# A differential attention whose values are computed with the queries on the partitions, and whose norm becomes a factor per partition

## The chip, the cores and the metric

The kernel runs on one core of one Trainium2 chip. The metric is the device time of one execution in microseconds; three runs of the kernel before gave 1177.27, 1177.3 and 1177.53, with a median of 1177.3 us. The engines named below are TensorE (PE, with its weight loads as PEld), VectorE (DVE), ScalarE (ACT), GpSimd (POOL) and SyncE (SP), which issues most of the DMAs.

## The reference, cut to what matters

The program is two transformer blocks over 512 tokens with a model width of 1024. The second block has a sparse attention of 8 heads and a differential attention of 4 heads. The change is in the differential attention, between the product with the values and the output projection:

```python
def rmsnorm(x, g):
    xf = x.astype(f32)
    y = xf * lax.rsqrt(jnp.mean(xf * xf, axis=-1, keepdims=True) + EPS)
    return (y * g.astype(f32)).astype(x.dtype)

# diff_attention, for a block of 128 queries; 4 heads, values of width 128
p = probs(q1, k1f) - lam * probs(q2, k2f)
o = jnp.einsum('bhqs,bshe->bqhe', p, vf)
...
o_d = rmsnorm(o_d, g_diff_sub[layer]) * (1.0 - lam_init)
mix = jnp.concatenate([o_a, o_d], axis=-1)
y = jnp.einsum('bsc,cd->bsd', mix, w_out[layer])
```

The norm is taken for each query and each head over the 128 columns of that head.

## The kernel before, in words

Every engine has a program written out by hand; the order of the work on an engine is the order of its code, and the engines meet at semaphores. Nothing is scheduled by a planner.

The attention stage (about 642 to 787 us of the span) is a loop over 32 tiles, `step(n)` for n from -2 to 32, which each engine has in its own version. Tiles 0 to 15 are the differential ones: head h = n // 4 and query block tb = n % 4, with (tb + 1) * 128 keys. Tiles 16 to 31 are pairs of sparse heads. In step n, TensorE computes the scores of tile n + 2 (L925), a part of a projection for the sparse attention (`project_part`, up to n = 16) or pieces of the output projection (`out2_piece`, from n = 20), transposes the probabilities of tile n (`turn`, L939) and multiplies those of tile n - 1 with the values (`values`, L963 for differential tiles, L967 for sparse ones). VectorE normalises tile n (`normalise`), and scales and masks the scores of tile n + 2 (`shift`, L1979); top-k work and rotary embeddings for later tiles lie between its steps. ScalarE copies the transposed probabilities out of PSUM (`keep_turned`, L1371) and takes the exponentials of tile n + 2 (`exp`, L1356). GpSimd splits each weight chunk of 128x1024 into a high and a low part (L411, L414) when TensorE has freed its slot, and computes the low part of heads 0 and 1 (`head_low2`, L462).

The outputs of one differential head are gathered in one PSUM bank, transposed: the 128 columns of the head on the partitions, the 512 queries along the free dimension. Since the norm is a mean over the partitions, it goes through TensorE. For head h:

- after its last tile, `keep_output` on ScalarE copies the bank to SBUF (`kept[h]`, L1381) and squares it (`sq`, L1383);
- `head_sums` on TensorE (L654, L656, at the end of steps 5, 9, 16 and 17) sums the squares of each query over the partitions with four matmuls of one column each, onto an eps that is scaled by the softmax totals; this gives four columns of the bank NB;
- `head_roots` on ScalarE (steps 9 and 17, two heads at a time) takes the roots from NB, and VectorE takes the reciprocals into `rn` (L2027, steps 12 and 18);
- `norm_spread` on TensorE (L677, at the steps of `SPREAD_AT`: 14, 15, 19, 20) turns each column of reciprocals into a row over all partitions of NB;
- VectorE multiplies `kept[h]` with the gain and with NB (L2032, same steps), into `kept[h]` for heads 0 and 1 and into NB for heads 2 and 3;
- ScalarE rounds the result to the high part `xh` (L1400, steps 16, 17, 19 and 20), and the low part `xl` is computed on GpSimd (heads 0 and 1) or on VectorE (L2017, steps 20 and 21).

NB is one bank: each user waits until the one before it has let go (semaphores `bc_used`, `xl_ready`).

## Time and profile before

| | |
|---|---|
| median of three runs | 1177.3 us |
| the profiled execution | 1177.28 us, of which the span of the trace is 1175.6 us |
| PE busy, of the span | 1156.2 us (98%) |
| DVE / ACT / POOL busy | 611.4 / 292.3 / 719.4 us |
| TensorE clock granted, mean | 0.996 of full |
| chain that ended last | PE 93%, DVE 5%, ACT 1%, issue 1% |

The profile gives one execution with the start and duration of every instruction. A step of the attention stage is found in it by its width: the scores and exponentials of block tb are (tb + 1) * 128 columns wide, so four widths come round for each head. Times below are from the start of the span; "idle before" is how long an engine had done nothing, followed by the instruction whose end let it go on.

### The profile page before, as it was taken

How to read it: one execution, taken by the hardware profiler on the slowest of the kernel's cores; microseconds unless marked ns; L12 is line 12 of the kernel's file. 1: busy time of each engine (PE TensorE's matmuls, PEld its weight loads, DVE VectorE, ACT ScalarE, POOL GpSimd, SP SyncE). 2: the span in 40 equal slices, each digit the busy share in tenths (PEclk: the TensorE clock that was granted, in tenths of full speed). 3: DMA queues.
4: the chain of work that ended last, by engine and by line, in shares of the span. 5: the costliest groups of instructions: out<-in, count | busy, mean ns of one | idle time of the engine just before them, and what ended most of it. 6: DMA issues, size and time to landing. Idle time of an engine off the chain costs nothing.

```text
span 1175.6 us, 15616 instructions
## 1 busy us (share of the span) xinstructions
PE 1156.2 (98%) x5400; PEld 931.0 (79%) x5400; DVE 611.4 (52%) x1001; ACT 292.3 (25%) x576; POOL 719.4 (61%) x440
## 2 busy tenths in 40 slices
PE   7999999999999999999999999999999999999997
PEld 5887788888888888888777776777888888888886
DVE  4989874540015444448689778847554001454114
ACT  5144162210002121120202346546421000221111
POOL 7879958656666566656556333225876666665660
PEclk9999999999999999999999999999999999999998
DMA  7321223323232232324342221112232232322312
GB/s 269 114 90 36 90 72 131 102 95 102 89 107 89 94 104 90 107 90 134 108 126 90 88 78 57 30 55 73 76 120 90 95 103 89 107 89 94 104 36 72
DMA packets 35761, 111.25 MB, mean 95 GB/s; under 512 B 4993, under 2 KB 7169, under 8 KB 35713
## 3 DMA queue, kind: packets, MB, share of 16 engines
q1 hardware_dynamic: 32352, 105.40, 27.2%
q10 hardware_dynamic: 3360, 5.21, 1.6%
q8 instruction: 30, 0.49, 0.2%
q14 instruction: 19, 0.15, 0.0%
HBM read 102.99 MB, written 2.10 MB: 89 GB/s over the span
## 4 chain that ended last, share of the span: by engine, by line
PE 93%; DVE 5%; ACT 1%; issue 1%; DMA 0%; DVEq 0%; SPq 0%; ACTq 0%
PE bank L560 26%; PE bank L562 25%; PE bank L561 25%; PE bank L925 2%; PE bank L591 2%; PE bank L593 2%; PE bank L592 2%; DVE bank L1596 2%; PE bank L625 1%; PE bank L617 1%; PE bank L939 1%; PE bank L618 1%; PE bank L967 1%; PE bank L883 1%; PE bank L963 1%
## 5 line engine op out<-in xcount | busy, mean ns | idle before, releaser
L414 POOL TENSOR_TENSOR wl<-raw,wh 128x1024 fp32r<-128x1024 f32 x188 | 455.1, 2421 | 15.7
L411 POOL TENSOR_SCALAR wh<-raw 128x1024 fp32r<-128x1024 f32 x188 | 203.1, 1080 | 391.9 <-PE bank L562 273.3
L560 PE MATMUL bank<-xh,wh 128*128 128x512 f32 x776 | 307.9, 397 | 0.4 <-ACT va L1332 0.4
L562 PE MATMUL bank<-xh,wl 128*128 128x512 f32 x776 | 302.4, 390 | 0.0
L561 PE MATMUL bank<-xl,wh 128*128 128x512 f32 x776 | 302.3, 390 | 0.0
L560 PE MATMUL bank<-uh,wh 128*128 128x512 f32 (+1 forms) x560 | 215.4, 385 | 0.0
L562 PE MATMUL bank<-uh,wl 128*128 128x512 f32 (+1 forms) x560 | 214.5, 383 | 0.0
L561 PE MATMUL bank<-ul,wh 128*128 128x512 f32 (+1 forms) x560 | 214.5, 383 | 0.0
L560 PEld LDWEIGHTS bank<-xh,wh 128*128 128x128 f32 x776 | 145.6, 188 | 45.6 <-issue 16.2
L1795 DVE TENSOR_TENSOR ul<-tmb,uh 128x512 f32 x64 | 124.6, 1947 | 90.2 <-ACT uh L1277 90.2
L562 PEld LDWEIGHTS bank<-xh,wl 128*128 128x128 f32 x776 | 145.6, 188 | 31.1
L561 PEld LDWEIGHTS bank<-xl,wh 128*128 128x128 f32 x776 | 145.8, 188 | 29.0 <-issue 0.2
L1276 ACT ACTIVATE tmb<-tmp 128x512 f32<-128x512 f32 x64 | 40.5, 633 | 413.1 <-DVE tmp L1792 413.1
L561 PEld LDWEIGHTS bank<-ul,wh 128*128 128x128 f32 x560 | 105.2, 188 | 20.9 <-issue 0.2
L560 PEld LDWEIGHTS bank<-uh,wh 128*128 128x128 f32 x560 | 105.2, 188 | 20.6 <-issue 0.2
L562 PEld LDWEIGHTS bank<-uh,wl 128*128 128x128 f32 x560 | 105.2, 188 | 20.6
L1792 DVE SCALAR_TENSOR_TENSOR tmp<-bank,rb 128x512 f32<-128x512 f32 x64 | 44.0, 688 | 70.7 <-PE bank L562 66.0
L1596 DVE SCALAR_TENSOR_TENSOR bank<-gpad,cols,bank 128x512 f32<-128x512 f32 x98 | 66.6, 744 | 0.0
L1806 DVE TENSOR_TENSOR x<-bank,x 128x512 f32 x8 | 5.5, 692 | 78.1 <-PE bank L562 78.1
L1808 DVE COPY y<-bank 128x512 f32 x8 | 5.5, 692 | 78.1 <-PE bank L562 78.1
L1277 ACT ACTIVATE uh<-tmp 128x512 f32 x64 | 39.6, 618 | 0.0
L591 PE MATMUL bank<-wh,xh 128*128 128x512 f32 x96 | 38.0, 395 | 0.0
(278 smaller groups left out, 1234.8 us busy)
## 6 DMA issues: line engine op xcount, KB each, us to landing
raw<-wstream SPq DMA_DIRECT2D x188, 512.0 KB, 3.3
x<-xT SPq DMA_DIRECT2D x8, 256.0 KB, 4.8
out<-x SPq DMA_DIRECT2D x16, 128.0 KB, 1.7
qi<-ropey ACTq DMA_DIRECT2D x16, 64.0 KB, 2.1
qd<-ropey ACTq DMA_DIRECT2D x16, 64.0 KB, 2.3
kd<-ropey ACTq DMA_DIRECT2D x16, 64.0 KB, 2.1
qa<-ropey SPq DMA_DIRECT2D x16, 64.0 KB, 2.0
ka<-ropey SPq DMA_DIRECT2D x16, 64.0 KB, 2.0
```

What stands on the lines that cost most here:

```text
L411: nc.gpsimd.tensor_scalar(wh[c][:], raw[c][:], 1.0, 1.0, ALU.mult, ALU.mult).then_inc(high_ready, 1)
L414: nc.gpsimd.tensor_tensor(wl[c][:], raw[c][:], wh[c][:].bitcast(F32), ALU.subtract).then_inc(split_ready, 1)
L560: mm(out, wh_, mh, start=start, stop=False)
L561: mm(out, wh_, ml, start=False, stop=False)
L562: return mm(out, wl_, mh, start=False, stop=stop)
L591: mm(out, xh[:, k, ts], wh[s][:, ws], start=k == 0, stop=False)
L592: mm(out, xh[:, k, ts], wl[s][:, ws], start=False, stop=False)
L1276: A(tmb[c][:], tmp[c][:], ACT.Square).then_inc(square_ready, 1)
L1277: A(uh[:, bass.ds(r * 4 + c, 1), :].rearrange("p a n -> p (a n)"), tmp[c][:], ACT.Square).then_inc(uh_ready, 1)
L1596: ins = V.scalar_tensor_tensor(out=out, in0=src, scalar=w, in1=acc, op0=ALU.mult, op1=ALU.add)
L1792: V.scalar_tensor_tensor(out=tmp[c][:], in0=bank[c][:], scalar=0.0, in1=rb[:], op0=ALU.max, op1=ALU.mult).then_inc(evacuated, 1)
L1795: V.tensor_tensor(ul[:, bass.ds(r * 4 + c, 1), :].rearrange("p a n -> p (a n)"), tmb[c][:], uh[:, bass.ds(r * 4 + c, 1), :].rearrange("p a ...
```

## The change

The product with the values is turned round: the transposed probabilities are now the stationary operand and the values the moving one, so that a bank holds the 128 queries of each block on the partitions and the columns of the head along the free dimension, once for each of the four query blocks. The mean over a head's columns is then a sum along the free dimension. ScalarE takes it with an accumulator output, in four squares of 128 columns for each head in place of one of 512. One small instruction on VectorE (`head_mean`, steps 9 and 17) adds the scaled eps for two heads; the root and the reciprocal follow, and VectorE multiplies each head with its reciprocals as a factor per partition (`natural_o`, steps 12, 13, 18 and 19). TensorE then transposes the head into NB (`head_turn`, at the steps where the spreads stood), and the gain, which is now again a factor per partition, is applied where NB is read: by ScalarE in a copy back to `kept[h]` for heads 0 and 1 (steps 14 and 15), and by the readers of NB for heads 2 and 3.

```diff
-            def head_sums(h):
-                at = 4 * (h % 2)
-                ...
-                mm(NB[:, at:at + TB], ident[:], scaled_eps[:, TB * h:TB * h + TB], start=True, stop=False)
-                for t in range(TB):
-                    last = mm(NB[:, at + t:at + t + 1], sq[h % 2][:, t * P:t * P + P], inv[:, 1:2],
-                              start=False, stop=t == TB - 1)
+            def head_turn(h):
+                pe.wait_ge(head_scaled, h + 1)
+                if h == 0:
+                    pe.wait_ge(bc_used, 8)
+                elif h < 3:
+                    pe.wait_ge(head_used, h)
+                else:
+                    pe.wait_ge(xl_ready, 3 * KT + 3)
+                for t in range(TB):
+                    last = nc.tensor.transpose(NB[:, t * P:t * P + P], kept[h][:, t * P:t * P + P], ident[:])
+                last.then_inc(head_turned, 1)
...
-                        last = mm(out, vd[:, j, h * P:h * P + P], pT[n % 2][0][:, b], start=j == 0, stop=j == tb)
+                        last = mm(out, pT[n % 2][0][:, b], vd[:, j, h * P:h * P + P], start=j == 0, stop=j == tb)
... TensorE, step(n)
-                if n in SPREAD_AT and SPREAD_AT[n] < 3:
-                    h = SPREAD_AT[n]
-                    pe.wait_ge(bc_used, 8 + h)
-                    norm_spread(8 + h)
+                if n in TURN_AT and TURN_AT[n] < 3:
+                    head_turn(TURN_AT[n])
...
-                if n in (5, 9):
-                    head_sums(n // 4 - 1)
-                if n in (16, 17):
-                    head_sums(n - 14)
... ScalarE, keep_output(h)
-                if h >= 2:
-                    act.wait_ge(sums_done, 6 + h)
                 A(kept[h][:], bank[1 if h == 3 else 6][:], ACT.Copy).then_inc(o_kept, 1)
                 act.wait_ge(o_kept, h + 1)
-                A(sq[h % 2][:], kept[h][:], ACT.Square).then_inc(head_sq, 1)
+                for t in range(TB):
+                    A(sq[h % 2][:, t * P:t * P + P], kept[h][:, t * P:t * P + P], ACT.Square,
+                      accum_out=head_sum[:, TB * h + t:TB * h + t + 1]).then_inc(head_sq, 1)
... ScalarE, step(n)
+                    if h < 2:
+                        act.wait_ge(head_used, h + 1)
+                        A(xh[:, 4 + h], kept[h][:], ACT.Copy).then_inc(xh_ready, 1)
+                    else:
+                        act.wait_ge(head_turned, h + 1)
+                        A(xh[:, 4 + h], NB[:], ACT.Copy, scale=diff_gain[:]).then_inc(xh_ready, 1)
                 if n + 2 < TILES:
                     exp(n + 2)
+                if n in TURN_AT and TURN_AT[n] < 2:
+                    h = TURN_AT[n]
+                    act.wait_ge(head_turned, h + 1)
+                    A(kept[h][:], NB[:], ACT.Copy, scale=diff_gain[:]).then_inc(head_used, 1)
... VectorE, step(n)
                 if 0 <= n < TILES:
                     normalise(n)
+                if n in (9, 17):
+                    b = n // 17 * 8
+                    dve.wait_ge(head_sq, 4 + b + 8)
+                    dve.wait_ge(eps_scaled, b // 4 + 2)
+                    V.scalar_tensor_tensor(out=sd[:, 0:8], in0=head_sum[:, b:b + 8], scalar=1.0 / P,
+                                           in1=scaled_eps[:, b:b + 8], op0=ALU.mult, op1=ALU.add).then_inc(head_mean, 1)
                 if n + 2 < TILES:
                     shift(n + 2)
                 if n in (12, 18):
...
-                    V.reciprocal(rn[:, 0:8], sd[:, 0:8]).then_inc(rn_ready, 2)
-                if n in SPREAD_AT:
-                    h = SPREAD_AT[n]
-                    dve.wait_ge(bc_done, 9 + h)
-                    V.scalar_tensor_tensor(out=kept[h][:] if h < 2 else NB[:], in0=kept[h][:], scalar=diff_gain[:],
-                                           in1=NB[:], op0=ALU.mult, op1=ALU.mult).then_inc(bc_used, 1)
+                    link(V.reciprocal(rn[:, 0:8], sd[:, 0:8]))
+                if n in (12, 13, 18, 19):
+                    h = n - 12 if n < 14 else n - 16
+                    natural_o = kept[h][:].rearrange("p (a b) -> p a b", a=TB)
+                    V.tensor_tensor(natural_o, natural_o, rn[:, h % 2 * TB:h % 2 * TB + TB].unsqueeze(2)
+                                    .to_broadcast([P, TB, P]), ALU.mult).then_inc(head_scaled, 1)
```

The low part of heads 2 and 3 is now computed from NB times the gain. Semaphore counts elsewhere fall by four, since four spreads are gone; no other order changes.

The order of the instructions moves at three places that matter. On ScalarE, steps 14 and 15 before, from the copy of tile 14's transposed probabilities (L1371) to the copy of tile 16's:

```order
L1371 ACTIVATE tmp_84<-bank 128x384 [waits turned,pv_done]
L1356 ACTIVATE probs_115,soft<-probs_115,soft 128x128 [waits shifted] x2
L1371 ACTIVATE tmb_87<-bank 128x512 [waits turned,pv_done]
L1356 ACTIVATE probs_122,soft<-probs_122,soft 128x256 [waits shifted]
L1356 ACTIVATE probs_123,soft<-probs_123,soft 128x256 [waits shifted]
L1371 ACTIVATE tmp_84<-bank 128x128 [waits turned,pv_done]
```

and now, where L1365 is that copy, L1350 the exponential and L1404 the new copy from NB:

```order
L1365 ACTIVATE tmp_84<-bank 128x384 [waits turned,pv_done]
L1350 ACTIVATE probs_116,soft<-probs_116,soft 128x128 [waits shifted] x2
L1404 ACTIVATE tmb_85<-bank,diff_gain 128x512 [waits head_turned]
L1365 ACTIVATE tmb_87<-bank 128x512 [waits turned,pv_done]
L1350 ACTIVATE probs_123,soft<-probs_123,soft 128x256 [waits shifted]
L1350 ACTIVATE probs_124,soft<-probs_124,soft 128x256 [waits shifted]
L1404 ACTIVATE tmb_86<-bank,diff_gain 128x512 [waits head_turned]
L1365 ACTIVATE tmp_84<-bank 128x128 [waits turned,pv_done]
```

Each of the two steps now ends with a read of NB, and TensorE's second turn waits for the first.

On VectorE, step 17 before, from the second half of the normalisation of tile 17 (L2007, L2008) over the shift of tile 19 (L1979) to the rotary products (L1502):

```order
L2007 RECIPROCAL soft<-soft 128x1 [waits exp_done]
L2008 TENSOR_SCALAR probs_123<-probs_123,soft 128x256 [waits dve_chain]
L1979 ISA probs_115,soft<-bank,work 128x512 [waits scores_done,turned]
L1979 ISA soft 128x1
L1979 ISA probs_115,soft<-bank,work 128x512 [waits scores_done]
L1979 ISA soft 128x1
L1502 TENSOR_TENSOR tmp_82<-bank,sinr 128x512 [waits chunk_done]
L1502 TENSOR_TENSOR tmp_83<-bank,cosr 128x512
```

and now, with the mean (L2023) in it:

```order
L2007 RECIPROCAL soft<-soft 128x1 [waits exp_done]
L2008 TENSOR_SCALAR probs_124<-probs_124,soft 128x256 [waits dve_chain]
L2023 SCALAR_TENSOR_TENSOR sd<-head_sum,scaled_eps 128x8 [waits eps_scaled,head_sq]
L1979 ISA probs_116,soft<-bank,work 128x512 [waits scores_done,turned]
L1979 ISA soft 128x1
L1979 ISA probs_116,soft<-bank,work 128x512 [waits scores_done]
L1979 ISA soft 128x1
L1502 TENSOR_TENSOR tmp_82<-bank,sinr 128x512 [waits chunk_done]
L1502 TENSOR_TENSOR tmp_83<-bank,cosr 128x512
```

The mean moved in ahead of the shift of tile 19, and it waits for `head_sq`, the squares of head 3.

On TensorE, from the values of tile 15 (L963) in step 16 to the sums at the end of step 17, before:

```order
L963 MATMUL bank<-tmb_87,vd 128x128 x3
L654 MATMUL bank<-scaled_eps,ident 128x4 [waits eps_scaled,head_sq,bc_used]
L656 MATMUL bank<-inv,sq_75 128x1 x4
L925 MATMUL bank<-ka,qa 128x512 [waits shifted] x2
L939 MATMUL bank<-ident,probs_122 128x128 [waits pT_ready,probs_ready]
L939 MATMUL bank<-ident,probs_122 128x128
L939 MATMUL bank<-ident,probs_123 128x128 [waits pT_ready,probs_ready]
L939 MATMUL bank<-ident,probs_123 128x128
L967 MATMUL bank<-tmp_84,va 64x128 [waits pT_ready,o_kept]
L967 MATMUL bank<-vd,va 64x128
L654 MATMUL bank<-scaled_eps,ident 128x4 [waits eps_scaled,head_sq]
L656 MATMUL bank<-inv,sq_76 128x1 x4
```

and now, where L964 and L968 are the values, L926 the scores and L940 the transposes:

```order
L964 MATMUL bank<-vd,tmb_87 128x128 x3
L926 MATMUL bank<-ka,qa 128x512 [waits shifted] x2
L940 MATMUL bank<-ident,probs_123 128x128 [waits pT_ready,probs_ready]
L940 MATMUL bank<-ident,probs_123 128x128
L940 MATMUL bank<-ident,probs_124 128x128 [waits pT_ready,probs_ready]
L940 MATMUL bank<-ident,probs_124 128x128
L968 MATMUL bank<-tmp_84,va 64x128 [waits pT_ready,o_kept]
L968 MATMUL bank<-vd,va 64x128
```

The two sums, L654 with the four one-column matmuls of L656, are gone, and nothing has taken their place.

## Rows read from the trace of the kernel before

**Rows 1.** PE by stretch: start:end, length, busy (instructions), granted clock, DMA share, GB/s.

```profile
645.00:700.00 55.00, 55.00 (x289) 1.00 0.26 77
...
710.00:715.00 5.00, 3.80 (x20) 1.00 0.34 110
```

**Rows 2.** Timeline of DVE, steps 11-14: start, us, engine, instruction, [idle before, releaser].

```profile
701.50 0.69 DVE L1883 TENSOR_TENSOR ropey<-tmp,tmp 128x512 f32<-128x512 f32 x1
...
705.06 0.56 DVE L1979 CUSTOM_DVE_ANT_0 probs<-bank,mask 128x384 f32<-128x384 f32 x1 [1.30 <-PE bank L925]
...
706.02 0.20 DVE L2027 RECIPROCAL rn<-sd 128x8 f32<-128x8 f32 x1
...
708.17 2.31 DVE L1997 SCALAR_TENSOR_TENSOR probs<-probs,soft 128x256 f32<-128x256 f32 x1
...
714.25 0.62 DVE L1997 SCALAR_TENSOR_TENSOR probs<-probs,soft,probs 128x384 f32<-128x384 f32 x1
```

**Rows 3.** Timeline of PE, steps 14 and 15.

```profile
714.92 0.55 PE L939 MATMUL bank<-ident,probs 128*128 128x128 f32 x3 [0.71 <-DVE probs L1997]
...
716.48 0.65 PE L677 MATMUL bank<-ident,rn 128*128 128x128 f32 x4
```

**Rows 4.** Timeline of DVE, steps 17 to 19.

```profile
725.37 0.69 DVE L1979 CUSTOM_DVE_ANT_0 probs<-bank,work 128x512 f32<-128x512 f32 x1 [1.95 <-PE bank L925]
...
727.99 0.42 DVE L2008 TENSOR_SCALAR probs<-probs,soft 128x384 f32<-128x384 f32 x1
...
729.38 1.71 DVE L1883 TENSOR_TENSOR ropey<-tmp,tmp 128x512 f32<-128x512 f32 x1
...
731.80 0.16 DVE L2007 RECIPROCAL soft<-soft 128x1 f32<-128x1 f32 x1
```

**Rows 5.** Timeline of PE, steps 18 and 19.

```profile
728.48 1.18 PE L939 MATMUL bank<-ident,probs 128*128 128x128 f32 x6 [0.18 <-DVE probs L2008]
...
732.70 1.08 PE L939 MATMUL bank<-ident,probs 128*128 128x128 f32 x8
```

**Rows 6.** PE by stretches of 1 us, steps 18 and 19.

```profile
730.00:731.00 1.00, 1.00 (x10) 0.50 0.00 0
...
732.00:733.00 1.00, 1.00 (x7) 0.66 0.00 0
```

**Rows 7.** Timeline of PE, step 5.

```profile
676.25 0.28 PE L654 MATMUL bank<-scaled_eps,ident 128*128 128x4 f32 x2
676.39 1.03 PE L656 MATMUL bank<-inv,sq 128*128 128x1 f32 x8
677.36 0.49 PE L925 MATMUL bank<-kd,qd 64*128 64x128 f32 x4
```

**Rows 8.** Timeline of ACT, steps 14 and 15, from the exponentials.

```profile
715.96 0.39 ACT L1356 ACTIVATE probs<-probs,soft 128x128 f32<-128x128 f32 x1
...
716.34 0.39 ACT L1356 ACTIVATE probs<-probs,soft 128x128 f32<-128x128 f32 x1
...
719.05 0.60 ACT L1371 ACTIVATE tmb<-bank 128x512 f32<-128x512 f32 x1 [2.23 <-PE bank L939]
```

**Rows 9.** Timeline of POOL, steps 12 and 18.

```profile
707.82 2.39 POOL L414 TENSOR_TENSOR wl<-raw,wh 128x1024 fp32r<-128x1024 f32 x1
...
729.27 1.27 POOL L462 TENSOR_TENSOR xl<-tmb,xh 128x512 fp32r<-128x512 f32 x1 [2.33 <-ACT xh L1400]
```

**Rows 10.** Source view of ACT's L1218, a copy with a scale: ns min/median/max.

```profile
L1218 ACT ACTIVATE vg<-bank,rn x4: 681/690/692, 77.6 to 79.5; 128x512 f32<-128x512 f32 x4
```

**Rows 11.** Timeline of ACT, steps 16 and 17, from the squares.

```profile
725.91 0.63 ACT L1383 ACTIVATE sq<-vd 128x512 f32<-128x512 f32 x1
...
730.51 0.72 ACT L1356 ACTIVATE probs<-probs,soft 128x512 f32<-128x512 f32 x1
```

**Rows 12.** Source view of ACT's L1159, squares without and with a scale.

```profile
L1159 ACT ACTIVATE sq<-x x24: 614/632/635, 161.9 to 829.4; 128x512 f32<-128x512 f32 x24
L1159 ACT ACTIVATE sq<-x,cols x8: 707/708/709, 440.5 to 516.5; 128x512 f32<-128x512 f32 x8
```

More of the change, by code:

```diff
@@ L1019, in step @@
                     turn(n)
-                if n in SPREAD_AT and SPREAD_AT[n] == 3:
-                    pe.wait_ge(xl_ready, 3 * KT + 3)
-                    norm_spread(11)
+                if n in TURN_AT and TURN_AT[n] == 3:
+                    head_turn(3)
                 if n >= 1:
                     values(n - 1)
-                if n in (5, 9):
-                    head_sums(n // 4 - 1)
-                if n in (16, 17):
-                    head_sums(n - 14)
             for n in range(-2, TILES + 1):
@@ L1531, in norm_factor @@
             def norm_factor(i, keep=None):
[L1533 removed]
+                dve.wait_ge(sd_ready, i + 1 if i < 8 else i + 3)
                 if i:
```

66 lines of the change are left out of this document (29 added, 37 removed).

## The prediction

> **What bounds the kernel now.** I read the busy time and the granted clock by stretch first, then the waits and the timeline of each engine for the attention stage, step by step. TensorE sets the end nearly everywhere. From 645 to 700 us it is busy for all of the 55.00 us at the full clock, and only in steps 12 to 14 does it show a hole, 3.80 us busy in 5 [rows 1]. So a microsecond taken from TensorE before 700 us is a microsecond off the end, and what the other engines do there is hidden unless it makes TensorE late. There are two places in this stage where TensorE follows somebody else, and both are in the way of the change.
>
> The first is steps 12 to 14. VectorE was idle for 1.30 us until TensorE's scores of tile 14 let it go at 705.06, and from there it runs without a pause to the probabilities of tile 14, which end at 714.87 [rows 2]. TensorE waits for them, 0.71 us, and starts its transposes at 714.92 [rows 3]. The second is steps 17 to 19. VectorE's shift of tile 19 starts at 725.37 as soon as TensorE's scores are there, its instructions then follow each other to 731.80, where the normalisation of tile 19 starts [rows 4], and TensorE's transposes start at 728.48, on a release by VectorE, and at 732.70 [rows 5]. TensorE's clock is down to half there: 0.50 from 730 to 731, 0.66 from 732 to 733 [rows 6]. After 733 us TensorE is the bound again. What the change costs or brings is therefore its effect on the start of the transposes of tile 19.
>
> **The change part by part: TensorE's sums of heads 0 and 1.** In step 5 the sums start at 676.25 and the next scores at 677.36 [rows 7], so one `head_sums` holds TensorE for 1.11 us. Those of heads 0 and 1 (steps 5 and 9) lie where TensorE never waits [rows 1]. Both go: -2.22 us. The values with swapped operands are the same number of matmuls of 128x128 on the same fp32 data, and the transposes of `head_turn` are four of the same 128x128 as those of `norm_spread`; both are taken at no change.
>
> **ScalarE's squares of heads 0 to 2** become four of 128 columns with an accumulator. I price them below; they cost well under 1 us more for a head, and at steps 4, 8 and 12 ScalarE next waits for TensorE's transposes, as it does for 2.23 us before 719.05 [rows 8]. Nothing. If that cover were gone they would cost 0.6 to 0.9 us for each head.
>
> **VectorE's factors of heads 0 and 1.** The mean in step 9 is one instruction of 8 columns, 0.2 us by the reciprocal of 8 columns [rows 2], and lies before a shift that waits for TensorE: nothing. In step 12 the reciprocal is now waited for (0.1 us) and a product of 128x512 follows. Its operands are all in SBUF; such a product took 0.69 us when alone [rows 2], and I charge 0.65, since the next instruction overlaps its end. That is 0.75 us on the chain to tile 13. But there the chain runs into GpSimd: the 256 columns of tile 13 took 2.31 us from 708.17, ending at 710.48, while 384 columns take 0.62 at 714.25 [rows 2], and GpSimd's split of a chunk ran until 710.21 [rows 9]. An SBUF-only instruction of VectorE stood until GpSimd was done. GpSimd is released by the same TensorE that releases VectorE, so both come 2.22 us earlier, and 0.75 us of arriving later at the same hold cost nothing. If the hold were not there, they would cost up to 0.75. The product of step 13 comes behind it and has no cover: +0.65 us on the start of the transposes of tile 14. The two products of VectorE that go, in steps 14 and 15, lie where TensorE does not wait for it: nothing back.
>
> **ScalarE's copies of heads 0 and 1.** TensorE turns head 1 in step 15, where its spread started at 716.48 [rows 3]. It now needs NB read, and the reader is ScalarE, behind the exponentials of tile 16. These start at 715.96 and 716.34, 0.38 apart [rows 8], so the copy starts at 716.72. A copy of 512 columns from PSUM with a scale per partition took 0.69 us [rows 10]. It ends at 717.41, and TensorE stands for 717.41 - 716.48 = 0.93 us with a projection, the transposes of tile 15 and all later work queued behind. All these times hang on the transposes of tile 14, so they shift together. From below, 0.8 (a copy as short as the 0.60 of the transposed tile [rows 8]); from above 1.0. I take +0.93. The copy of head 1 has 2 us of idle time around it and costs nothing.
>
> At the start of step 16 this makes -2.22 + 0.65 + 0.93 = **-0.64 us**.
>
> **Steps 16 to 19.** The sums of heads 2 and 3 go too, 2.22 us of TensorE's time. But the mean of heads 2 and 3 stands on VectorE ahead of the shift of tile 19, and it waits for the last square of head 3. ScalarE starts these squares at 725.91 [rows 11], since head 3's output comes late, after the exponentials of tile 18. One square of 512 columns without a scale takes 0.63 us, with one 0.71 [rows 12]; exponentials of 128 columns, with a pointer and an accumulator, follow each other every 0.38 us [rows 8]. Without the pointer (0.08 less) four squares take 4 x 0.30 = 1.2 us, with it 1.5. I take 1.25. VectorE gets on at 725.91 + 1.25 + 0.2 for the mean = 727.4, where the shift stood at 725.37: **2.0 us later** (1.8 to 2.4). Behind the mean are queued the shift of tile 19, for which TensorE's scores of tile 20 wait, then the rotary products and the normalisation of tile 18, for which its transposes wait. What TensorE saved in steps 16 and 17 it spends standing there: the saving is worth nothing.
>
> In step 18 the awaited reciprocal and the product of head 2 add 0.1 + 0.65 = 0.75 us ahead of the rotary sum and the normalisation of tile 19. GpSimd's hold, 1.27 us from 729.27 [rows 9], made the rotary sum at 729.38 last 1.71 us [rows 4]; it follows ScalarE's rounding of head 1, which comes 0.6 us later, and meets the normalisation of tile 18 instead, due at 727.99 + 2.0 = 730.0 [rows 4]. It is paid once either way. So the normalisation of tile 19 starts at 731.80 + 2.0 + 0.75 = 734.55, and its first half is ready about 0.65 us on (reciprocal, and a factor over 512 columns), at 735.2, where the transposes of tile 19 began at 732.70 [rows 5]: **+2.5 us**. ScalarE is no rival to that: its exponentials of tile 19 move from 730.51 [rows 11] by only 0.6. From there TensorE has no wait that the new order adds: the gain on NB makes the low part an instruction of the same length, and for heads 2 and 3 VectorE's product between spread and rounding is gone, which gives slack but no time.
>
> **The clock.** TensorE now stands for some 3 us between the values of tile 16 and the scores of tile 20, and again before tiles 18 and 19. In before, where it stood for far less between small matmuls, the clock was at half rate for some 3 us, about 729.5 to 732.7 [rows 6], and a half-rate stretch costs half its length where TensorE is the bound. If one ends before 735.2 it is hidden; if it begins there it costs 1.6. I take +0.7.
>
> The Trainium skill (TensorE: Matmul & The Clock Gate, section HAM oscillation — how this bites in real kernels) has the rule that standing sends the array to half rate and that the work after the gap then starts cold. That rule speaks against this change, and by it the full 1.6 us would fall due, for a time of 1180.7 us; the trace of before shows such a dip, but not where it falls when the gap is longer.
>
> **The sum.** -0.64 + 2.5 + 0.7 = +2.56 us. The profiled execution took 1177.28 us, 1.7 more than its span of 1175.6; the median of the runs is 1177.3. So 1177.28 + 2.56 = **1179.8 us**.
>
> **Rivals.**
>
> *The wait in step 17 is covered, not slower.* If head 3's squares were done before VectorE comes to the mean, the sums of all four heads count: -4 x 1.11 + 0.65 + 0.93 = -2.9 us, 1174.4 us. This decides if the squares end by 725.4. For it speaks that ScalarE was idle before step 16 and that TensorE gets to head 3's values earlier in its own order; against it, that the squares stood at 725.91 with nothing between them and their input but the exponentials of tile 18 [rows 11], so they would have to come 1.8 us earlier.
>
> *The cost of the wait is smaller.* Squares as quick as 0.25 us, no dip of the clock behind step 19 and TensorE's transposes of tile 18 and scores of tile 21 catching up: 1.2 less for the clock and squares, and with the copies at their lower bound about +0.6, 1177.9 us. What speaks for it is that the half-rate time of before also cost something in these steps and may be spared now.
>
> *The clock stays down and the squares are long.* Four squares at 0.38 (+0.3), step 12's product not covered (+0.6) and 1.6 in place of 0.7 for the clock: +4.4, 1181.7 us. The dip of before [rows 6] speaks for it; GpSimd's hold speaks against the second part.
>
> **Chances.** Forecast 0.57, its own range 1178.8 to 1181.0; covered wait 0.08; smaller cost 0.18; clock and long squares 0.17. The range to hold the time 8 times in 10 is 1175.8 to 1182.6. A difference of 0.2% (2.35 us) is about what a measurement tells from no change: the bounds are 1174.95 and 1179.65. The forecast lies just above the upper one, so about 0.33 of its 0.57 counts as slower, with all of the last case: slower 0.50, within 0.42, faster 0.08.
>
> **What would show it.** Right: in the trace of after, VectorE's mean of step 17 has some 2 to 4 us of idle time before it, released by ScalarE's squares; TensorE waits about 0.9 us in step 15 on ScalarE's copy, and a few microseconds in step 18 on VectorE; everything to step 11 stands 2.2 us earlier; the transposes of tile 19 start near 732.70 - 0.64 + 2.5 = 734.6, and from there to the end the shift is constant up to the clock. Wrong: no wait at the mean (then faster), a shift at step 11 that is not 2.2 us, values with swapped operands that take another time, or a half-rate stretch in steps 20 and 21 or none at all.

## The result: 1181.6 us, slower by 0.37%

| | before | after |
|---|---|---|
| median (runs) | 1177.3 us (7) | 1181.62 us (7), 1181.2 to 1182.71 |
| profiled execution | 1177.28 us, span 1175.6 | 1182.71 us, span 1181.0 |
| ratio of the times | | 1.0037, 95% interval 1.0028 to 1.0046 |

The prediction was 1179.8 us with a range of 1175.8 to 1182.6. The direction and the range held; the forecast's own range (1178.8 to 1181.0) did not. By the medians the difference is 4.3 us and in the profiled executions 5.4 us, where the sum said 2.56. The profiled execution of after is the slowest of its seven, 1.1 us above the median and just outside the range. What follows explains that execution. Four of the seven lie at 1181.2 to 1181.62 with a mean granted clock of 0.994 to 0.996, three at 1182.17 to 1182.71 with 0.993 to 0.994. That agrees with a part of the half-rate time below being there in some executions and not in others.

The page of after, its first lines: span, and busy time of each engine. TensorE has 40 instructions less and is busy 1.4 us less, in a span that is 5.4 us longer: it stands idle 6.8 us more. The four sums that are gone were 4.4 us of its work, so some 3 us of the 1154.8 are the same work at a lower clock (an estimate from these two numbers).

```profile
span 1181.0 us, 15563 instructions
...
PE 1154.8 (98%) x5360; PEld 929.6 (79%) x5360; DVE 611.9 (52%) x1003; ACT 296.2 (25%) x606; POOL 718.6 (61%) x440
```

TensorE in after by stretch (length, busy, granted clock, DMA), for [rows 1] and [rows 6]. The stretch to 700 us now has a hole of 1.05 us, and there are two stretches at half rate (a granted clock of 0.50 is 1.2 GHz, 1.00 is 2.4 GHz) where before had one: 3.4 us from 717 to 721 and 6.8 us from 731 to 738, against 3.4 in before (the length is the clock that is missing in each microsecond, divided by a half and added up).

```profile
645.00:700.00 55.00, 53.95 (x273) 1.00 0.27 82
...
717.00:718.00 1.00, 0.53 (x3) 0.68 0.00 0
718.00:719.00 1.00, 1.00 (x5) 0.50 0.06 16
...
731.00:732.00 1.00, 0.87 (x3) 0.51 0.01 4
736.00:737.00 1.00, 1.00 (x8) 0.50 0.00 0
737.00:738.00 1.00, 1.00 (x7) 0.58 0.00 0
```

The timeline of TensorE in after, its waits in steps 10 to 19 (start, duration, instruction, idle time before it and who ended it), for [rows 3] and [rows 5]. L940 are the transposes of a tile's probabilities (tiles 10, 13, 14, 15, 18 and 19 here), L658 those of `head_turn`, L926 the scores.

```profile
698.27 0.55 PE L940 MATMUL bank<-ident,probs 128*128 128x128 f32 x3 [1.05 <-DVE probs L1997]
...
709.86 0.44 PE L940 MATMUL bank<-ident,probs 128*128 128x128 f32 x2 [0.49 <-DVE probs L1997]
...
714.85 0.55 PE L940 MATMUL bank<-ident,probs 128*128 128x128 f32 x3 [1.30 <-DVE probs L1997]
...
717.47 1.09 PE L658 MATMUL bank<-ident,tmb 128*128 128x128 f32 x4 [0.99 <-ACT tmb L1404]
...
720.86 0.60 PE L940 MATMUL bank<-ident,probs 128*128 128x128 f32 x4
...
730.61 1.40 PE L926 MATMUL bank<-ka,qa 64*128 64x128 f32 x4 [2.92 <-DVE soft L1979]
733.98 1.54 PE L940 MATMUL bank<-ident,probs 128*128 128x128 f32 x6 [1.97 <-DVE probs L2008]
...
738.22 1.04 PE L940 MATMUL bank<-ident,probs 128*128 128x128 f32 x8
```

VectorE in after, for [rows 2] and [rows 4]. L2023 is the new mean: VectorE stands 3.17 us ahead of it in step 9 and 3.82 us in step 17, until ScalarE's squares are there. The two long L1997 and the long L2008 ran beside an instruction of GpSimd: those of 695.83 and 732.47 beside the two shown below, that of 708.15 beside L417 from 707.14 to 709.53.

```profile
692.60 0.17 DVE L2023 SCALAR_TENSOR_TENSOR sd<-head_sum,scaled_eps 128x8 f32<-128x8 f32 x1 [3.17 <-ACT sq L1376]
...
695.83 2.38 DVE L1997 SCALAR_TENSOR_TENSOR probs<-probs,soft 128x384 f32<-128x384 f32 x1
...
708.15 1.66 DVE L1997 SCALAR_TENSOR_TENSOR probs<-probs,soft 128x256 f32<-128x256 f32 x1
...
729.73 0.17 DVE L2023 SCALAR_TENSOR_TENSOR sd<-head_sum,scaled_eps 128x8 f32<-128x8 f32 x1 [3.82 <-ACT sq L1376]
...
732.47 1.46 DVE L2008 TENSOR_SCALAR probs<-probs,soft 128x384 f32<-128x384 f32 x1
```

GpSimd in after, for [rows 9].

```profile
695.41 2.38 POOL L417 TENSOR_TENSOR wl<-raw,wh 128x1024 fp32r<-128x1024 f32 x1
...
732.45 1.26 POOL L465 TENSOR_TENSOR xl<-tmb,xh 128x512 fp32r<-128x512 f32 x1 [3.02 <-ACT xh L1395]
```

ScalarE in after: the first and the last of head 3's four squares, and the table load behind them, for [rows 11]. They follow each other every 0.30 us, 728.42 to 729.70.

```profile
728.42 0.31 ACT L1376 ACTIVATE sq<-vd 128x128 f32<-128x128 f32 x1
...
729.31 0.29 ACT L1376 ACTIVATE sq<-vd 128x128 f32<-128x128 f32 x1
...
729.72 1.28 ACT L1416 ACT_TABLE_LOAD   x1
```

The best single ruler is ScalarE's copy of each tile's transposed probabilities, which follows TensorE closely. Its start, minus that of the same tile in the kernel before (us; the kernels of the other columns come in the next section, "repairs" is the kernel with three repairs):

| tile | after | mean moved | copies on VectorE | no sums | repairs | repairs, filled |
|---|---|---|---|---|---|---|
| 5 | +0.04 | -0.08 | +0.22 | +0.03 | +0.46 | +0.24 |
| 6 | -0.99 | -1.11 | -0.80 | -0.87 | -0.57 | -0.79 |
| 10 | -0.77 | -2.15 | -0.58 | -1.77 | -1.62 | -1.84 |
| 14 | -0.07 | -1.45 | +0.10 | -1.80 | -1.52 | -1.74 |
| 15 | +2.50 | -0.40 | +0.12 | -1.80 | -1.37 | -1.59 |
| 17 | +3.15 | +0.25 | +0.77 | -1.80 | -0.72 | -0.94 |
| 19 | +5.46 | +0.99 | +3.89 | -1.06 | -0.06 | -0.84 |
| 22 to 28 | +5.4 | +1.4 | +3.9 | -1.0 | -0.1 | -0.7 |

The row of tile 5 is a start-up difference of the execution; a column is read down from it. Each column is one execution of its kernel.

### The profile page after: what moved, and what is told of

It reads as the page before. It is cut to its first block, busy times and chain, and to the rows that moved or that the text cites. A ratio compares the mean times of both kernels' runs of the same rounds, so it can differ in the third digit from the quotient of the medians.

```text
span 1181.0 us, 15563 instructions
## 1 busy us (share of the span) xinstructions
PE 1154.8 (98%) x5360; PEld 929.6 (79%) x5360; DVE 611.9 (52%) x1003; ACT 296.2 (25%) x606; POOL 718.6 (61%) x440
## 4 chain that ended last, share of the span: by engine, by line
PE 92%; DVE 5%; ACT 1%; issue 1%; DMA 0%; DVEq 0%; SPq 0%; ACTq 0%
PE bank L563 25%; PE bank L565 25%; PE bank L564 25%; PE bank L594 2%; PE bank L596 2%; PE bank L595 2%; DVE bank L1596 2%; PE bank L926 2%; PE bank L628 1%; PE bank L940 1%; PE bank L620 1%; PE bank L621 1%; PE bank L968 1%; PE bank L884 1%; PE bank L964 1%
## 5 line engine op out<-in xcount | busy, mean ns | idle before, releaser
L417 POOL TENSOR_TENSOR wl<-raw,wh 128x1024 fp32r<-128x1024 f32 x188 | 454.5, 2417 | 15.7
L414 POOL TENSOR_SCALAR wh<-raw 128x1024 fp32r<-128x1024 f32 x188 | 203.0, 1080 | 397.4 <-PE bank L565 278.2
```

The source lines that it names most:

```text
L414: nc.gpsimd.tensor_scalar(wh[c][:], raw[c][:], 1.0, 1.0, ALU.mult, ALU.mult).then_inc(high_ready, 1)
L417: nc.gpsimd.tensor_tensor(wl[c][:], raw[c][:], wh[c][:].bitcast(F32), ALU.subtract).then_inc(split_ready, 1)
```

## The experiments

Theory 1, formed from the trace of after: VectorE's in-order wait for ScalarE's squares at the mean loses the saving of step 9 and costs 2 us in step 17. Rival A: the squares on ScalarE themselves are the cost, wherever the mean stands. Rival B: TensorE's clock in step 15 falls whatever waits there. Rival C: VectorE is the engine that is late in steps 14 and 15. The kernel before ran beside each kernel; its median was 1177.3 to 1177.5 us each time.

**mean_late.** The mean of both steps goes behind the shift:

```diff
@@ VectorE, step(n)
-                if n in (9, 17):
-                    ... the mean into sd, two waits ahead of it
                 if n + 2 < TILES:
                     shift(n + 2)
@@ VectorE, the loop over n, behind qk_second
+                if n in (9, 17):
+                    ... the same lines
```

> The changed kernel with VectorE's mean of steps 9 and 17 behind the shift (and behind the second rotary part or the score's maxima) of the same step. Theory 1 (VectorE's in-order wait for ScalarE's squares, ahead of a shift that TensorE and ScalarE wait for, lost the saving of step 9, about 1.0 us, and cost 2.0 us in step 17, and pushed step 18's instructions under GpSimd's hold and into the half-rate stretch, up to 2.3 us more): the median falls from 1181.6 to between 1176.5 and 1178.7 us; tile 10 to 13 stand 1.8 us ahead of the kernel before instead of 0.8. Rival A (the squares themselves on ScalarE, four of 0.3 us in place of one of 0.7, are the cost, wherever the mean stands): 1181 to 1182. Rival B (TensorE's clock stays low after the wait of head_turn(1) in step 15 and that alone makes the loss): at most 0.5 us less, 1181.1 or more.

Measured: 1179.19 us (1178.31 to 1180.77, 11 runs), ratio to before 1.0017 (1.0008 to 1.0026): 2.4 us back. Tiles 10 to 13 stand 2.1 us ahead of before (expected 1.8). Rivals A and B, each as the whole cause, fall; but the time is above the range of theory 1. What is left shows in TensorE's timeline: step 14 waits 1.32 us for VectorE, step 15 0.99 us for ScalarE's copy, and in step 18 the wait did not go. It changed its owner, from VectorE to ScalarE. The clock, 1.00 at 717, does not fall behind the wait of step 15 in this execution, which is one of the quicker ones (1178.64 us, mean clock 0.995); four of the eleven took 1180.03 to 1180.77 us at 0.993 to 0.994, as they would with one such stretch more.

```profile
713.48 0.55 PE L940 MATMUL bank<-ident,probs 128*128 128x128 f32 x3 [1.32 <-DVE probs L1997]
...
716.09 0.63 PE L658 MATMUL bank<-ident,tmb 128*128 128x128 f32 x4 [0.99 <-ACT tmb L1404]
...
728.73 1.51 PE L940 MATMUL bank<-ident,probs 128*128 128x128 f32 x6 [2.91 <-ACT tmb L1365]
```

**mean17_late.** The mean of step 17 alone is moved.

> The changed kernel with the mean of step 17 alone behind that step's shift; step 9 as in the changed kernel. Theory 1: the 2.0 us of step 17 come back, and of step 18's 2.3 us what hangs on it; 1177.5 to 1179.7 us, and about 1 us more than with both moved. Rival A (squares) and B (clock after step 15): within 0.5 us of 1181.6.

Measured: 1180.03 us (1179.37 to 1181.57, 11 runs), ratio 1.0022 (1.0013 to 1.0031). So step 17 gives 1.6 us back and step 9 another 0.8, the order that theory 1 has, but 0.3 us above its range. TensorE's wait of 1.06 us before the transposes of tile 10 is still there, as it was in after.

**copies_dve.** ScalarE's copies of heads 0 and 1 go to VectorE, everything else as in after:

```diff
@@ ScalarE, step(n)
-                if n in TURN_AT and TURN_AT[n] < 2:
-                    ...
-                    A(kept[h][:], NB[:], ACT.Copy, scale=diff_gain[:]).then_inc(head_used, 1)
@@ VectorE, step(n), behind shift and the reciprocals
+                if n in TURN_AT and TURN_AT[n] < 2:
+                    h = TURN_AT[n]
+                    dve.wait_ge(head_turned, h + 1)
+                    V.tensor_scalar(kept[h][:], NB[:], diff_gain[:], None, ALU.mult).then_inc(head_used, 1)
```

> The changed kernel with the copies of heads 0 and 1 out of NB (times the gain) on VectorE in steps 14 and 15, ahead of nothing that TensorE waits for, in place of ScalarE. Theory 1 with the forecast's step (TensorE's head_turn(1) waits 0.99 us for ScalarE's copy, which stands behind an exponential): the copy comes earlier by 0.5 to 1 us, TensorE's wait of step 15 goes below 0.5 us, and if the half-rate stretch at 717 to 721 us hangs on that wait it goes too; median 1178.5 to 1181.0. Rival B (the clock falls there whatever waits): the wait goes, the clock stays at half rate, 1180.7 to 1181.7. Rival C (VectorE is the engine that is late there, so 0.4 us more on it in steps 14 and 15 costs as much as ScalarE gives): 1181.5 to 1183.

Measured: 1180.81 us (1180.54 to 1181.52, 7 runs), ratio 1.0028 (1.0017 to 1.004): 0.8 us less than after, and rival C falls. The time alone would also fit rival B; the trace decides against it. In it far more happened: TensorE's wait of step 15 is gone, its clock is 1.00 from 717 to 721, and tile 15 stands 2.4 us earlier than in after. Both the 0.99 us and, in the traced executions, the 1.6 us at half rate hung on ScalarE's copy. But a part, 0.8 us, is given back between tiles 17 and 19, where the mean and GpSimd's hold are still in the way: behind a wait for the mean, L2004 of tile 18 is held again.

```profile
727.35 0.17 DVE L2019 SCALAR_TENSOR_TENSOR sd<-head_sum,scaled_eps 128x8 f32<-128x8 f32 x1 [3.82 <-ACT sq L1376]
...
730.09 1.46 DVE L2004 TENSOR_SCALAR probs<-probs,soft 128x384 f32<-128x384 f32 x1
```

**no_sums.** The kernel before without the matmuls that sum the squares:

```diff
@@ TensorE, head_sums(h)
-                mm(NB[:, at:at + TB], ident[:], scaled_eps[...], start=True, stop=False)
-                for t in range(TB):
-                    last = mm(NB[:, at + t:at + t + 1], sq[h % 2][...], inv[:, 1:2], ...)
+                last = mm(NB[:, at:at + TB], ident[:], scaled_eps[...], start=True, stop=True)
```

> The kernel before with the sixteen one-column matmuls that sum the squares of the four heads left out (the norm's factor is then computed from epsilon alone). It prices what the change removes from TensorE with nothing put in its place. Theory (in-order TensorE waits for its own work in steps 5 and 9, each 1.0 to 1.1 us, in steps 16 and 17 as well if nothing else is late there): 2.0 us less at step 10, and 2 to 4 us less at the end: 1173.3 to 1175.3. Rival (waits for VectorE and ScalarE behind those steps take the saving back): 1176 to 1177.3.

Measured: 1176.3 us (1175.25 to 1177.18, 11 runs), ratio 0.9987 (0.9978 to 0.9996). The saving is 1.0 us of the 4 us of work removed (1.03 for each head by [rows 7]). In the trace it is 1.8 us up to step 10, near the 2.0 foreseen; in steps 16 and 17 it is nothing, and between tiles 18 and 19 0.8 us go back. Its timeline of TensorE says why: where the sums were, it waits for ScalarE.

```profile
724.80 0.39 PE L654 MATMUL bank<-scaled_eps,ident 128*128 128x4 f32 x2 [1.30 <-ACT sq L1380]
...
726.68 1.51 PE L936 MATMUL bank<-ident,probs 128*128 128x128 f32 x6 [1.07 <-ACT tmb L1368]
```

And its clock falls around the second of these waits and stays down for 6.8 us instead of 3.4 (TensorE by stretches of 1 us, first, second and last of the half rate):

```profile
725.00:726.00 1.00, 0.60 (x6) 0.77 0.76 266
...
726.00:727.00 1.00, 0.32 (x2) 0.50 0.56 225
...
732.00:733.00 1.00, 1.00 (x10) 0.82 0.44 107
```

The 0.8 us do not go back in every execution: five of the eleven took 1175.25 to 1175.57 us at a mean clock of 0.996 to 0.998, 1.8 to 2.1 us less than before, and six took 1176.3 to 1177.18 at 0.995 to 0.996, the traced one among them.

This gave **theory 2**: from step 16 to step 18 ScalarE is the bound, already in the kernel before. From 723.25 to 735 us of the trace of before it has no idle time; two exponentials of 384 columns, head 3's copy and squares, a table load, the copies of tile 17 and a second table load follow each other. The sums lay in TensorE's wait for it and, by this theory, kept the clock up. Then, in after, the four squares, 1.28 us where one took 0.63 [rows 11], are paid in full, and an idle TensorE pays again in clock. (The copy of tile 17 is that of its transposed probabilities.)

**fixed** has three repairs: mean_late, copies_dve, and the product of head 1 in step 14 instead of 13 (`if n in (12, 14, 18, 19)`).

> The changed kernel with all three repairs on VectorE's side: the mean of steps 9 and 17 behind the shift, the copies of heads 0 and 1 on VectorE, and the product of head 1 in step 14 instead of 13. Theory 2 (in steps 16 to 18 ScalarE, busy without a gap from 723 to 736 us, is what TensorE waits for, and the four squares of head 3 make its chain 0.65 us longer than before): up to tile 16 the whole saving stands, 2.0 us, at tile 18 1.3 to 1.4 us are left, and TensorE's half-rate stretch, 6.5 us long in the kernel with the mean moved and 3.3 us before, takes another 1.0 to 1.4 us: median 1176.8 to 1178.0. Rival (theory 1 alone: the waits that were repaired were the whole loss, nothing of the kind is left behind them): 1175.0 to 1175.7.

Measured: 1177.16 us (1176.86 to 1178.01, 11 runs), ratio 0.9997 (0.9988 to 1.0006): no difference to before, and 4.5 us less than after. Theory 2's number and its course fit, the rival's 1175.7 does not (the lowest run is 1176.86): read from tile 5 on, it is 2.1 us ahead at tile 10, 1.8 at tile 15, 1.2 at tile 17 and 0.5 at tile 19. The wait in step 18 is 2.92 us for ScalarE's copy of tile 17:

```profile
727.76 1.51 PE L940 MATMUL bank<-ident,probs 128*128 128x128 f32 x6 [2.92 <-ACT tmb L1365]
```

and the half rate runs from 726 to 733:

```profile
726.00:727.00 1.00, 0.00 (x0) 0.62 0.94 373
...
732.00:733.00 1.00, 1.00 (x7) 0.50 0.27 66
```

**fixed_fill** adds five matmuls of 512 columns, whose result nobody reads, in that wait:

```diff
@@ TensorE, step(n), behind scores(n + 2)
+                if n == 18:
+                    pe.wait_ge(head_used, 2)
+                    for _ in range(5):
+                        mm(NB[:], ones[:], mask[:], start=True, stop=True)
```

> The kernel with the three repairs, and five matmuls of 512 columns by constants into the free bank NB, computed for nothing, on TensorE in step 18 behind scores(20), in the wait for ScalarE. Theory 2 (an idle TensorE in that wait brings the half-rate stretch forward and makes it longer; the one-column sums that the change removed had kept it busy there): the stretch starts later or is shorter by 2 us or more, and the median is 0.6 to 1.2 us below that of the three repairs alone. Rival (the stretch comes whatever TensorE does there): no gain, 0 to 0.3 us more.

Measured: 1176.6 us (1176.29 to 1176.72, 11 runs), ratio 0.9991 (0.9982 to 1.0): 0.56 us less than without them, and no run of one kernel reaches into those of the other. The gain is just below the 0.6 to 1.2 expected, since the five (4.56 us) overrun the wait: turn(18) starts at 728.95 where ScalarE had released it at 727.4. No stretch of the trace is below full clock, which is more than was expected; the mean clock is 0.997 to 0.999 in all eleven runs and 0.995 in all eleven of fixed, and the runs lie within 0.43 us instead of 1.15.

```profile
724.55 4.56 PE L1014 MATMUL bank<-mask,ones 128*128 128x512 f32 x10
728.95 0.82 PE L940 MATMUL bank<-ident,probs 128*128 128x128 f32 x6
...
731.86 1.25 PE L940 MATMUL bank<-ident,probs 128*128 128x128 f32 x8 [0.28 <-DVE probs L2008]
```

**sums_head3** is the kernel before with the sums of head 3 alone kept.

> The kernel before with the one-column matmuls of heads 0, 1 and 2 left out and those of head 3 kept (the norm's factor of the three is then computed from epsilon alone). Theory 2 (in step 17 these sums lie in a wait for ScalarE and only keep TensorE's clock up): 0.6 to 0.9 us faster than with all four left out, that is 1175.3 to 1175.7, with a half-rate stretch of 3 to 5 us instead of 6.4. Rival (they cost their 1.0 us in step 17 too): 1 us slower than with all left out, 1177.3.

Measured: 1175.42 us (1175.24 to 1177.15, 11 runs), ratio 0.9986 (0.9977 to 0.9995). With 1.0 us more of work for TensorE than no_sums it is not slower: the lowest runs are 1175.24 and 1175.25, and the traced executions 1175.32 and 1176.3. So the sums of head 3 cost nothing, and the rival (1177.3) falls. In these two traces the same transposes start at the same time but here at full clock (0.85 us in place of 1.51), and the half rate is 727 to 731:

```profile
726.68 0.85 PE L939 MATMUL bank<-ident,probs 128*128 128x128 f32 x6 [0.18 <-ACT tmb L1371]
```

The medians differ by 0.9 us, but that is which of two groups the middle run fell in. Here eight runs took 1175.24 to 1175.87 us (mean clock 0.996 to 0.998) and three 1176.59 to 1177.15 (0.995); in no_sums five and six. The means are 1175.8 and 1176.1 and the intervals overlap, so that the small sums make the long stretch rarer is not shown.

**fixed_one** puts one square for each head back on ScalarE, with two reductions on VectorE ahead of each mean (`reduce_sum` of `sq[h]` as 128x4x128 into four columns of `head_sum`). ScalarE also waits for the first mean ahead of the squares of heads 2 and 3.

> The kernel with the three repairs, and ScalarE's four squares of 128 columns with sums per head put back to one square of 512 columns; VectorE sums them (two reductions of 128x4x128) just ahead of the mean. Theory 2: ScalarE's chain in step 16 gets 0.65 us shorter, so turn(18) starts 0.6 us earlier and the median falls by 0.5 to 0.8 us against the three repairs alone, unless the two reductions (0.6 us each) on VectorE, behind the second rotary part in step 17, delay turn(18) by as much: turn(18) would then wait for VectorE. Rival (ScalarE's squares are not on the path): no change or 0.3 us more.

Measured: 1178.12 us (1177.38 to 1178.52, 11 runs), ratio 1.0005 (0.9996 to 1.0014): 1.0 us slower than fixed. The exception in the expectation came true, so this says nothing against theory 2. Two reductions take 1.40 us in line, and turn(18) now waits for VectorE; in step 9 the other two push the normalisation of tile 10 (L1993 here) under GpSimd's hold again (2.29 us, and TensorE waits 1.06).

```profile
726.29 1.40 DVE L2060 TENSOR_REDUCE head_sum<-sq 128x4 f32<-128x512 f32 x2
...
728.47 1.54 PE L940 MATMUL bank<-ident,probs 128*128 128x128 f32 x6 [2.76 <-DVE probs L2004]
```

**one3_fill** keeps that for head 3 alone (one square, one reduction in step 17), on the kernel with three repairs and four filling matmuls.

> The kernel with the three repairs and the matmuls of constants in step 18 (four instead of five), and for head 3 alone one square of 512 columns on ScalarE with one reduction of 0.7 us on VectorE behind the second rotary part, in place of four squares with sums. The reduction for head 3 lies where VectorE waited for ScalarE (0.36 us), so little is late behind it. Theory 2 (ScalarE's chain from step 16 on sets turn(18) and turn(19)): 0.3 to 0.7 us below the 1176.6 us of the kernel with four squares and matmuls of constants. Rival (VectorE is the bound there as well, by its products and GpSimd's hold): within 0.2 us of 1176.6.

Measured: 1176.3 us (1176.06 to 1177.24, 11 runs), ratio 0.9990 (0.9981 to 0.9999); 0.3 us below fixed_fill, which was measured beside other runs of before (medians 1177.37 and 1177.45); the ratios to before, 0.9990 and 0.9991, hardly differ. At tile 17 it is 0.6 us better than fixed_fill, both read from tile 5, as theory 2 has it, but at turn(19) 0.3 is left: the rival is right there. (Turn(18) itself is no test, since in both kernels it follows the filling matmuls, five of them in one and four in the other.) VectorE's rotary sum is held by GpSimd and turn(19) waits for VectorE:

```profile
728.24 1.76 DVE L1885 TENSOR_TENSOR ropey<-tmp,tmp 128x512 f32<-128x512 f32 x1
...
731.46 1.25 PE L940 MATMUL bank<-ident,probs 128*128 128x128 f32 x8 [0.81 <-DVE probs L2010]
```

**piece_fill** fills the wait with needed work, the first piece of the output product out of step 20, between one and two filling matmuls (`PIECES = {18: 1, 19: 0, 20: 1, 21: 2, ...}`).

> The kernel with the three repairs, where TensorE's wait of step 18 (2.9 us) is filled with work that is needed: the first piece of the output product (three matmuls of 512 columns, 0.7 to 0.8 us) is moved from step 20 to step 18, with one matmul of constants ahead of it and two behind. Theory 2 (the wait is for ScalarE, and TensorE is the bound again from step 20 on, so work moved into the wait is saved): 0.5 to 0.8 us below the 1176.6 us of the kernel filled with constants alone. Rival (step 20 has a wait of its own that takes it back): 1176.4 to 1176.8.

Measured: 1176.35 us (1176.09 to 1176.5, 11 runs), ratio 0.9989 (0.9980 to 0.9998), 0.25 us below fixed_fill (with the same reservation as above), half of the least that was expected and just below the rival's 1176.4. turn(19) cannot start before ScalarE has copied tile 18 and VectorE has normalised tile 19, so a part of the piece's time came back as a wait:

```profile
731.90 1.25 PE L940 MATMUL bank<-ident,probs 128*128 128x128 f32 x8 [1.23 <-ACT vd L1371]
```

**best** joins the two, with one filling matmul on each side of the piece.

> Both of these together (one square for head 3, the first piece of the output product in step 18, one matmul of constants ahead of it and one behind). Theory 2: the two add up, 1175.2 to 1175.8. Rival: 1176.2 or more, the bound of the steps 18 and 19 being VectorE and GpSimd's hold.

Measured: 1177.0 us (1175.84 to 1177.16, 11 runs), ratio 0.9990 (0.9981 to 1.0). The two do not add up, as the rival had it. Turn(19) starts at 731.38, as early as in no other kernel with the change, but TensorE has then stood 1.75 us for VectorE, and the clock is at half rate from 733 us on:

```profile
731.38 1.25 PE L940 MATMUL bank<-ident,probs 128*128 128x128 f32 x8 [1.75 <-DVE probs L2012]
```

```profile
733.00:734.00 1.00, 1.00 (x11) 0.51 0.45 109
...
736.00:737.00 1.00, 1.00 (x7) 0.78 0.29 72
```

Its lowest run is the lowest of all kernels with the change; its median is not. Five of its runs took 1175.84 to 1176.14 us at a mean clock of 0.998 to 0.999, six 1177.0 to 1177.16 at 0.996 to 0.997. That agrees with such a stretch being there or not, but only one execution, of the second group, has a trace.

**before_piece** is the kernel before with the piece moved and nothing else.

> The kernel before with the first piece of the output product moved from step 20 to step 18, and nothing else: it says how much of a gain of the two kernels above has nothing to do with the change. In the kernel before TensorE waits only 0.18 us in step 18 but its clock falls right behind. Theory 2: the piece takes time there that TensorE does not have, 0 to 0.5 us gained through the clock: 1176.9 to 1177.6. Rival (the wait for ScalarE is there too, hidden by the sums): 0.6 us faster or more, 1176.7 or less.

Measured: 1177.31 us (1177.09 to 1177.72, 11 runs), ratio 0.9996 (0.9987 to 1.0005): nothing. Its trace says more than its time. The clock is 1.00 from 725 to 735 us, where before has its 3.4 us at half rate [rows 6], and still tile 19 is not earlier, since TensorE, done sooner, waits for VectorE:

```profile
729.06 0.82 PE L939 MATMUL bank<-ident,probs 128*128 128x128 f32 x6
...
732.57 1.23 PE L939 MATMUL bank<-ident,probs 128*128 128x128 f32 x8 [0.90 <-DVE probs L2008]
```

So the half-rate stretch of before cost next to nothing: with it these transposes began at 732.70 [rows 5]. The runs of before agree, with medians of 1177.4 to 1177.5 us at a mean clock of 0.996 and 1177.3 to 1177.4 at 0.998. So the gain of the filled kernels is not one that the kernel before could have had from the piece alone. Whether filling matmuls would have helped it was not tried.

The versions that beat both kernels are piece_fill and one3_fill, by 1.0 us or 0.1% against before, with intervals that end just below 1. Of what was tried, the change is worth that much at most, and only with three repairs and a filled wait.

## Why the prediction was right in direction and short in size

Against the profiled execution, by the steps of the sum (us; measured from the table of shifts). It is the slowest of seven; against the median the sum is short by 1.8 us instead of 2.9:

| step | forecast | measured |
|---|---|---|
| sums of heads 0 and 1 | -2.22 | -0.8 |
| product of step 13 | +0.65 | +0.7 |
| step 15, TensorE waits for ScalarE's copy | +0.93 | +2.6, of it 0.99 wait, 1.6 half rate |
| steps 16 to 19, and the clock | +2.5 and +0.7 | +3.0 |
| sum | +2.56 | +5.46 |

**The step that failed** is "The mean in step 9 [...] lies before a shift that waits for TensorE: nothing". The shift does wait for TensorE, as the one in step 12 does [rows 2], but ScalarE's squares of head 1 end later than that wait: with the mean ahead of it the shift started at 692.72, and in mean_late, without, at 691.18, 1.4 us earlier when both are read from tile 5. So everything at step 11 stood 0.8 us earlier and not 2.2, which the prediction had named as a sign of being wrong. In step 17 the same mechanism was seen and priced, in step 9 it was not looked for. The price was raised by the neighbour: L1997 of tile 10 began 0.42 us behind GpSimd's instruction of 2.38 us instead of ahead of it, and TensorE waited 1.05 us. mean_late has 1.3 us at tile 10 that mean17_late does not have, and no wait there. The other 0.1 us of the difference is the size of the sums: without the mean in the way the two were worth 2.1 us and not 2.22.

**The clock** was right in kind and misplaced. The forecast put +0.7 behind the start of tile 19's transposes. There was no loss there (the shift is constant from tile 19 on), but 1.6 us in step 15, behind a wait of 0.99 us that followed one of 1.30 us, and a stretch of 6.8 us in steps 18 and 19. copies_dve shows the first (wait gone, clock at 1.00, 2.4 us back). For the second, fixed_fill shows that filling the wait takes the stretch away. The rule of the Trainium skill in the prediction (TensorE: Matmul & The Clock Gate, section HAM oscillation — how this bites in real kernels), that work behind a gap starts cold, agrees in kind with both: head_turn at 717.47 took 1.09 us where the same four took 0.66 at 711.50. It did not say which of these gaps, shorter than the 3 to 5 us of its own case, would be followed by such a stretch. In mean_late the same two waits in steps 14 and 15 (1.32 and 0.99 us) were followed by none, and what decides is open.

**Step 17** was right in place and price: four squares took 1.28 us (forecast 1.25), and the shift of tile 19 came 4.48 us later than in before, of which 2.50 were there already: 1.98, forecast 2.0. GpSimd's hold did meet the normalisation of tile 18, as said (1.46 us for 0.42), but "paid once either way" overlooked that this one is on the path to turn(18), and that is one more wait of TensorE, 1.97 us, in a stretch at half rate. VectorE's own path came out as forecast: its normalisation of tile 19 began at 737.03, that is 2.73 us later than in before once the 2.50 are taken off, where 2.75 was forecast, and its first half was done at 737.71. But TensorE, late from turn(18) and at half rate, got to turn(19) only at 738.22 and without a wait. So the last 0.5 us is a path that the prediction did not have.

**The saved sums of heads 2 and 3** were rightly called worth nothing, for a reason that reaches further than the one given: not the new wait alone, but ScalarE, which sets steps 16 to 18 in the kernel before too (no_sums). The rival "covered wait", 1174.4 us, was therefore no possible outcome: no_sums, with all sums gone and nothing in their place, never came below 1175.25, and fixed, with the mean's wait gone, still gave 1177.2.

**Product, copy, swapped operands.** The product of step 13 (+0.7) and the wait for ScalarE's copy (0.99) came as priced, the product of step 12 was hidden under GpSimd's hold but for 0.1 us (L1997 at 708.15, ended by 709.81), and the values with swapped operands take 1.06 us for eight matmuls, as before.

**The other two rivals.** "The clock stays down and the squares are long" gave 1181.7 us, which is the median measured, but by chance: the squares took 0.30 us each and not 0.38, the product of step 12 cost 0.1 and not 0.6, and the clock's 1.6 us fell in step 15. "The cost of the wait is smaller" counted on the half-rate time of before to be worth something; before_piece shows that it was not. That the range held is in part luck too, since the 1.3 us lost in step 9 and the clock of step 15 were in none of its cases.

## What to carry to other kernels

Price a removed instruction by what its engine would do in its place: if it would wait, the removal is worth nothing, and on TensorE it may cost, since an idle wait can be followed by a stretch at half rate (fixed against fixed_fill, 0.56 us). A stretch at half rate has a price only where TensorE is what the others wait for: that of before had none. An in-order wait that is added must be checked at every place where it stands, also where the instruction behind it waits anyway: the two releases have to be compared in time, with the savings of the same change already applied to one of them. When work goes to an engine with 25% load, look at its timeline in the step concerned; ScalarE was idle three quarters of the span and without a pause for these 12 us.

## What the runs showed of the hardware that was not expected

- Waits of 1 to 3 us of TensorE, and in before two of 0.41 and 0.18 us with the small sums between them, were followed by 3.4 or 6.8 us at 1.2 GHz, while it was working again; waits of 0.81 to 1.23 us in one3_fill, before_piece and piece_fill, and of 1.32 and 0.99 in mean_late, were not. With five matmuls of constants in a wait of 2.9 us there was none (fixed against fixed_fill). The two kernels that fill the wait fully, fixed_fill and piece_fill, also have the narrowest times: 0.4 us over 11 runs, the other variants 0.6 to 2.5.
- VectorE and GpSimd hold each other, in both directions. L1997 over 384 columns takes 0.62 us alone and 2.38 us from 695.83, ending 0.4 us after GpSimd's L417; L465 takes 1.26 us alone and 1.49 to 1.76 when VectorE's product of head 2 is already running (1.49 in mean_late, 1.76 in one3_fill). The three MAX8 of step 9 (1.48 us from 693.94, GpSimd's L414 from 694.29) and the shift out of PSUM in before (0.69 us, as always, with L462 from 725.68) ran at their length beside GpSimd. The Trainium skill (Advanced Engine Details and Errata, section Miscellaneous Facts) says that the two share a read and a write interface, and that VectorE's instructions with two SBUF inputs or in a two-port mode conflict; the traces agree.
- Four squares of 128 columns with an accumulator cost ScalarE 1.28 us, one of 512 without 0.63; the sum over the same columns costs VectorE 0.70 us as a reduction. In fixed, with the mean out of the way, they still cost 0.65 us in step 16 (tile 16 to tile 17 in the table).
